# Second mixer: the state-space activation runs two passes later, the convolution's high part behind the tables, and one gate product ahead of the first linear part

## The reference

```python
y_ssm  = s5_mixer(u, ...)        # gelu(scan's output), then y @ w_glu: linear part and gate
y_conv = short_conv_mixer(...)   # (gate_b * causal_conv(gate_c * x)) @ w_out
y_attn = nsa_mixer(...)          # compressed, selected and windowed attention, @ w_o
gates  = sigmoid(mix_gates).reshape(bsz, seq, 3, D_MODEL)
mixed  = gates[:, :, 0] * y_ssm + gates[:, :, 1] * y_conv + gates[:, :, 2] * y_attn
x = x + mixed @ w_out
```

## Time and profile before

| what | us |
|---|---|
| time, median of 3 executions | 1519.97 (1518.13 to 1520.04) |
| profiled execution, its own time | 1513.86 |
| its span in the trace | 1511.9 |
| second mixer's passes and what follows up to `lin0`, in the trace | 1085 to 1234 |

### The profile page before, as it was taken

One profiled execution on the slowest core, in us unless ns is written; L12 is line 12 of the kernel. 1 busy time (PEld: TensorE's weight loads), 2 busy tenths in 40 slices (PEclk: granted clock), 3 DMA queues, 4 the chain that ended last, 5 costly groups with the idle time before them and its releaser, 6 DMA issues.

```text
span 1511.9 us, 24315 instructions
## 1 busy us (share of the span) xinstructions
PE 1464.1 (97%) x8495; PEld 1269.4 (84%) x8495; DVE 1146.9 (76%) x1836; ACT 771.6 (51%) x1257; POOL 140.1 (9%) x140
## 2 busy tenths in 40 slices
PE   6999999999999999999999999999999999999998
PEld 5888889888888888888978888798777789888887
DVE  4777777877777778777787777867599877568776
ACT  5443466563444543446655434467588665453432
POOL 0000015100000000004220000010332310000000
PEclk9999999999999999999999999999899999999999
DMA  7566545546565666565455665456222246646652
GB/s 294 196 196 195 191 148 175 154 152 193 197 194 187 208 204 188 191 194 152 142 167 190 195 194 187 167 172 227 98 84 70 85 145 190 186 156 193 195 192 81
DMA packets 71072, 261.74 MB, mean 173 GB/s; under 512 B 8016, under 2 KB 8016, under 8 KB 70736
## 3 DMA queue, kind: packets, MB, share of 16 engines
q1 hardware_dynamic: 69696, 253.79, 52.0%
q10 hardware_dynamic: 1296, 6.85, 1.3%
HBM read 259.56 MB, written 1.05 MB: 172 GB/s over the span
## 4 chain that ended last, share of the span: by engine, by line
PE 87%; DVE 6%; ACT 4%; issue 2%; POOL 1%; DMA 0%; DVEq 0%; ACTq 0%
PE work L733 24%; PE work L734 12%; PE work L469 8%; PE work L470 8%; PE work L471 8%; PE acc L469 7%; PE acc L471 7%; PE acc L470 7%; DVE wlo L455 2%; ACT whi L448 1%; PE work L1458 1%; PE acc L1487 0%; DVE x L572 0%; ACT xboth L526 0%; DVE frac L1868 0%
## 5 line engine op out<-in xcount | busy, mean ns | idle before, releaser
L455 DVE TENSOR_TENSOR wlo<-raw,whi 128x1024 fp32r<-128x1024 f32 x460 | 548.7, 1219 | 195.0 <-ACT whi L448 193.6
L733 PE MATMUL work<-xboth,whi 128*128 128x512 f32 x1600 | 560.7, 393 | 0.0
L448 ACT ACTIVATE whi<-raw 128x1024 fp32r<-128x1024 f32 x480 | 475.8, 1040 | 49.0 <-PE work L471 35.2
L734 PE MATMUL work<-xboth,wlo 128*128 128x256 f32 x1600 | 445.3, 278 | 0.0
L733 PEld LDWEIGHTS work<-xboth,whi 128*128 128x128 f32 x1600 | 299.7, 187 | 68.6
L734 PEld LDWEIGHTS work<-xboth,wlo 128*128 128x128 f32 x1600 | 301.1, 188 | 4.3
L813 ACT ACTIVATE sg<-sg 128x256 f32<-128x256 f32 x100 | 41.8, 418 | 476.0 <-DVE sg L854 476.0
L471 PE MATMUL acc<-whi,hlo 128*128 128x512 f32 x440 | 173.8, 395 | 0.0
L470 PE MATMUL acc<-wlo,hhi 128*128 128x512 f32 x440 | 173.6, 395 | 0.0
L469 PE MATMUL acc<-whi,hhi 128*128 128x512 f32 x440 | 173.5, 394 | 0.0
L469 PE MATMUL work<-xboth,whi 128*128 128x256 f32 x488 | 143.2, 293 | 0.0
(11 more groups left out here) (433 smaller groups left out, 2069.5 us busy)
## 6 DMA issues: line engine op xcount, KB each, us to landing
raw<-stream SPq DMA_DIRECT2D x480, 512.0 KB, 3.7
par<-pm ACTq DMA_DIRECT2D x2, 1644.5 KB, 7.3
pfa<-pf_a ACTq DMA_DIRECT2D x3, 516.0 KB, 3.9
pfb<-pf_b ACTq DMA_DIRECT2D x2, 516.0 KB, 8.1
x<-x_in SPq DMA_DIRECT2D x2, 512.0 KB, 5.8
out<-x SPq DMA_DIRECT2D x2, 512.0 KB, 2.6
par<-pm ACTq DMA_DIRECT2D x1, 820.0 KB, 4.7
pre<-pf_a ACTq DMA_DIRECT2D x1, 4.0 KB, 4.0
```

What stands on the lines that cost most here:

```text
L448: nc.scalar.activation(chunk(whi, place, c)[:, cols], chunk(raw, place, c)[:, cols], ACT.Copy).then_inc(hi_ready, 1)
L455: nc.vector.tensor_tensor(chunk(wlo, place, c)[:, cols], chunk(raw, place, c)[:, cols], chunk(whi, place, c)[:, cols].bitcast(F32), ALU.su ...
L733: nc.tensor.matmul(o[:, :], hi[:, k * P:(k + 1) * P], xboth[:, k, :], start=k == 0, stop=False)
L734: m = nc.tensor.matmul(o[:, 0:S], lo[:, k * P:(k + 1) * P], xhi[:, k, :], start=False, stop=k == KD - 1)
```

## The change

Three edits. `s5_gelu(k)` moves from the end of passes 4, 8 and 12 to passes 6, 10 and 14, where it stands behind the exponentials and ahead of the tables; DVE's `y5lo` moves with it, from passes 5, 9, 13 to 7, 11, 15. `cvhi` moves from behind the exponentials to behind the tables and the `cv` copy of the same pass. And `EARLY` takes in an 18th gate, e17, which is block (5, 2): PE computes it between `ot3` and `lin0`, into the spare bank, with its own copy, `split_hi` and `split_lo`; `g52` goes from the late part. The weight stream is re-ordered to match.

```diff
-EARLY = [(i, b) for i in range(KD) for b in range(3)][:17]
+EARLY = [(i, b) for i in range(KD) for b in range(3)][:18]
...
-BANKED2 += _tail + _ots
...
+BANKED2 += _tail + _ots + ["e17"]
...
+BY_ACT2 += _tail + ["e17"]
 BY_DVE2 += _ots
@@ mix2_pe
                 done(f"ot{b}", m)
+            early(17)
             for i in range(KD):
@@ mix2_act
                 emptied(f"sc{r}", ins)
-                if 3 <= r <= 12 and r % 3 == 0:
-                    vec2.wait(act, BY_DVE2.index(f"cv{r - 1}") + 1)
-                    cv_hi.inc(nc.scalar.activation(cvhi[:, r // 3 - 1, :], cvt[:, :], ACT.Copy))
                 if r == 0:
                     job2.wait(act, JOB2["pct"])
                     copy("pct", pcT[:, :, :].rearrange("p t n -> p (t n)"), bank2("pct", slice(0, S)))
+                if r >= 6 and r % 4 == 2:
+                    s5_gelu(r // 4 - 1)
                 if t == 0 and h + 1 < 8:
                     tables(h + 1)
...
+                if 3 <= r <= 12 and r % 3 == 0:
+                    vec2.wait(act, BY_DVE2.index(f"cv{r - 1}") + 1)
+                    cv_hi.inc(nc.scalar.activation(cvhi[:, r // 3 - 1, :], cvt[:, :], ACT.Copy))
                 split_hi(act, place, SPLIT_AFTER[r])
-                if r >= 4 and r % 4 == 0:
-                    s5_gelu(r // 4 - 1)
...
                 o_hi.inc(nc.scalar.activation(ohi[:, b, :], bank2(f"ot{b}", slice(0, S)), ACT.Copy))
+            early(17)
@@ mix2_dve
-                if r % 4 == 1 and r > 1:
+                if r % 4 == 3 and r > 4:
                     s5_low(r // 4 - 1)
...
                 emptied(f"ot{b}", ins)
+            split_lo(dve, place, [E_CHUNK[17] + 6])
```

More of the change, by code:

```diff
@@ L66 @@
 D_B = [D_ROUNDS + c for c in (3, 8, 13, 18)]
-E_CHUNK = [D_MIXED + c for c in (2, 5, 8, 11, 12, 13, 14, 15)] + [D_ROUNDS + c for c in (15, 16, 17, 19, 20, 21, 22, 23, 24)]
+E_CHUNK = [D_MIXED + c for c in (2, 5, 8, 11, 12, 13, 14, 15)] + [D_ROUNDS + c for c in (15, 16, 17, 19, 20, 21, 22, 23, 24, 25)]
 SPLIT_AFTER = {0: [6], 1: [7], 2: [8], 3: [9, 10], 4: [11], 5: [12], 6: [13], 7: [14, 15], 8: [16], 9: [17],
@@ L75 @@
     for _name in [f"g{_i}{_b}" for _b in range(3) if (_i, _b) not in EARLY] + [f"lin{_i}", f"br{_i}"]:
-        LATE[_name] = D_ROUNDS + 25 + len(LATE)
-D_PAD = D_ROUNDS + 25 + len(LATE)
+        LATE[_name] = D_ROUNDS + 26 + len(LATE)
+D_PAD = D_ROUNDS + 26 + len(LATE)
 D_OUT = D_PAD + 1
@@ L184 @@
 _tail = ["pt15", "e12", "e13", "e14", "e15", "e16"]
-BANKED2 += _tail + _ots
-BANK2.update(zip(_tail + _ots, [TURNED, CHANNEL, SPARE, SCORES, INPUTS, CHANNEL, TURNED, SCORES, INPUTS, CHANNEL]))
-BY_ACT2 += _tail
+BANKED2 += _tail + _ots + ["e17"]
+BANK2.update(zip(_tail + _ots + ["e17"], [TURNED, CHANNEL, SPARE, SCORES, INPUTS, CHANNEL, TURNED, SCORES, INPUTS, CHANNEL, SPARE]))
+BY_ACT2 += _tail + ["e17"]
 BY_DVE2 += _ots
@@ L325, in block_program @@
         gx = sb("gx", [P, 4, S])
-        gates32 += [gx[:, j, :] for j in range(3)] + [xn[:, t, 512:768] for t in range(T)]
+        gates32 += [gx[:, j, :] for j in range(3)] + [xn[:, t, 512:768] for t in range(T)] + [xn[:, 0, 768:D]]
         mxhi, mxlo = sb("mxhi", [P, KD, S], F32R), sb("mxlo", [P, KD, S], F32R)
@@ L2409, in mix2_chunks @@
     chunks.update(zip(E_CHUNK, [mg[b * KD + i] for i, b in EARLY]))
-    parts += [chunks[c] for c in range(D_MIXED, D_ROUNDS + 25)]
+    parts += [chunks[c] for c in range(D_MIXED, D_ROUNDS + 26)]
     def half(v, i):
```

## The result

Four executions of the changed kernel took 1507.78 to 1510.3 us, median 1509.57; four of the kernel before 1516.52 to 1520.04, median 1519.05. The ratio is 0.9939 (95% interval 0.9927 to 0.9952), 9.5 us by the medians. Measured again later beside 23 executions of the kernel before, it was 1511.04 against 1519.04, ratio 0.9946 (0.9933 to 0.9959), 8.0 us. The profiled execution of the changed kernel took 1507.78 us with a span of 1506.1, 6.1 us less than the profiled one of before. Of the 5.8 us between the spans, 3.9 us lie between nm(1) and `lin0` and 3.1 us behind `lin0`, less 1.2 us ahead of nm(1), where the changed kernel's execution was the later one.

What follows compares the result with a forecast made beforehand. DVE was taken to bound the middle passes and PE alone everything from `lin0` on. Gate 2.9 plus passes 4.9 gave 7.8 us, so 1519.97 - 7.8, say 1512 us, with a forecast range of 1510.5 to 1514.5 (chance 0.60).

Steps and rivals of the forecast that it cites:

- The bound and the gate: Ahead of `lin0`, where PE alone sets the time after: the gate fills the 3.19 us gap, worth 2.9 us, 3.2 at most.
- The last four us: Passes 12 to 15: DVE's 4.22 us wait for nm(15) goes; the passes give 3.4 to 5.5 us, 4.9 taken.
- The thin cover: Pass 14: exp(15) ends at 1205.2 to 1205.9, just ahead of PE's transposes at 1206.0; half a microsecond more would count.
- exp(13) comes 4.0 us earlier: End of pass 12: exp(13) starts at about 1190.2 instead of 1194.19, about 0.4 us behind nm(13).
- The expected price of pass 10: Three table loads: PE stands about 3.3 us in pass 11; half clock, likelier than not, costs pass 12 1.5 to 2.9 us.
- a sign of being wrong: Passes 8 and 12: a wait of DVE for scores(8) or scores(12) of over 1 us would show the prediction wrong.
- The early waits give nothing, DVE is busy there anyway: Passes 4 and 8: removing the early gelu's waits, and moving DVE's `y5lo` (0.4 us each), gains nothing.
- The difference of 6.11 us between the profiled execution and the median: Whole kernel: the profiled execution lay 6.11 us under the median; the same difference was set on the forecast median.
- more than forecast: Rival, whole kernel: clock stays up and unprofiled executions now lose more to late exponentials; 1508.5 to 1510 us, chance 0.06.
- `cvhi` as a term of its own: Pass 12: `cvhi` out of the way brings ACT's work up to the split 2.6 us earlier; no separate time gain given.
- The drain: ACT in passes 6 and 10: skill's rule of about 1380 ns per table switch, 4.1 us more each; left out of sum.
- slower with ACT as the bound: Rival, passes 6 and 10: ACT's list becomes the longest and delays DVE; with 5.5 us per pass, 1523 us, chance 0.06.

Runs made afterwards that it cites:

- e1: Only the 18th gate kept; activations and `cvhi` back in their old places, against the changed kernel; 1514.54 us against 1518.25 for the kernel before, ratio 0.9981.
- e2: The 18th gate put ahead of the transposes, so the wait for `olo` stays, activations and `cvhi` as before; 1520.85 us against 1518.25 before, ratio 1.0018.
- e3: The moves of all three activations and of `cvhi`, without the 18th gate (17 gates); 1514.96 us against 1518.25 before, ratio 0.9981.
- e4: Against the kernel before, 17 gates: `cvhi` moved and only the last activation moved, pass 12 to 14; 1515.04 us against 1518.25, ratio 0.9979.
- e8: Only the three activations moved against the kernel before, `cvhi` still behind the exponentials, 17 gates; 1517.75 us against 1519.04, ratio 0.9992.
- e9: The kernel before, unaltered, profiled a second time; 1518.71 us, span 1516.9, where its first profiled execution took 1513.86.
- e7: Only `cvhi` moved behind the tables against the kernel before, activations unmoved, 17 gates; 1518.77 us against 1519.04, ratio 0.9992.
- e5: The changed kernel unaltered, measured again beside the kernel before on the same chip; 1511.04 us against 1519.04, ratio 0.9946.
- e11: e10's version with `cvhi` back behind the exponentials; 1511.57 us against 1517.65 for the kernel before, ratio 0.9962.
- e6: The changed kernel with the three activations at the end of passes 5, 9 and 13, behind the split; 1507.58 us against 1519.04 before, ratio 0.9927.
- e10: The same version as e6, measured again; 1506.9 us against 1517.65 for the kernel before, ratio 0.9929.

## Why the prediction came out as it did

**The bound and the gate: right.** `lin0` waits 0.32 us where 0.3 were left over, the gate takes its place, and e1 and e2 show that the filled wait is what pays. The term of 2.9 us was measured at 2.9 to 3.7. Its upper bound of 3.2 left out the clock that may fall behind the gap: e2, e3, e4 and e8 had 1.4 to 2.4 us more to lose there, though neither profile of before had.

**The last four us: right in kind.** The 4.22 us wait of DVE went, scores(14) follow values(12) without a wait (1195.46 after 1194.97), the chain through POOL's rotation and the last `states_out` moved as one, and no wait appeared at the last transposes. The thin cover held: exp(15) end at 1209.1 and the transposes that need them start at 1209.46. The size in the profiled pair is 3.7 us from nm(1) to nm(15) (113.95 to 110.2) and 3.9 us from nm(1) to `lin0` (140.0 to 136.1), inside 3.4 to 5.5 and under the 4.9 taken, since the half clock behind PE's stand in pass 11 came in all three traces of this order (e3, the changed kernel twice). The stand itself was foreseen (3.3 us expected, 1.12 + 1.67 measured) and half clock was called likelier than not, yet the sum took a value near the end without it.

**"exp(13) comes 4.0 us earlier": not reached.** It starts 2.0 us behind the end of nm(13) (1194.01 against 1192.02), not 0.4. The expected price of pass 10 is the cause: with pass 12 at half clock, PE's transposes, not ACT, hold `pT`(12) (a wait of 2.48 us). In e4, where PE does not stand in pass 11, exp(13) comes 0.46 us behind nm(13), as forecast, and from nm(1) to nm(15) it takes 4.8 us less than e9. DVE is later in e3 than in e4 by 1.2 us from nm(11) to nm(15), where I had next to nothing: it waits 0.65 us for scores(12) and 1.03 us for the state inputs behind them. The prediction had named a wait of over 1 us there as a sign of being wrong.

**"The early waits give nothing, DVE is busy there anyway": wrong in most of the traces.** It was read from one execution, in which it was true. In four of the six traces of kernels that keep the early activations (e2, e4, e7 and e9; not in e1 and the first of before) the low clock behind PE's stands in passes 5 and 9 lasts longer, and DVE waits 0.9 to 1.1 us at nm(7) and 1.5 to 1.6 us at nm(11). In the first profiled pair the passes and the gate make 3.7 + 2.9 = 6.6 us. From e9 to the changed kernel it is 116.1 to 110.2 us, so 5.9 between nm(1) and nm(15), and with the gate's 2.9 it makes 8.8, against 8.0 and 9.5 measured. Moving those activations removed that wait, and put another in pass 12 in its place: 2.5 us less and 1.2 us more in e3 than in e4. The 0.7 us that are left of it at `lin0` are too little for the medians to show.

**The difference of 6.11 us between the profiled execution and the median: set on wholesale, and wrongly.** Some 2.2 us of it lie in the passes and are touched by the change. The rival "more than forecast" (1508.5 to 1510) named this, with 0.06, and the first median, 1509.57, lay in it; e5's 1511.04 lay in the forecast's own 1510.5 to 1514.5. That 7.8 us come so near to the measured 8.0 is in part luck: the price in pass 12 was set too low and the early waits at nothing, and the two errors work against each other.

**`cvhi` as a term of its own: mis-seen.** The prediction counted 2.6 us of ACT for it in pass 12 and put it with the activation into one term, without a price for either alone. In pass 6 it saw only that the gap for the convolution hides the activation. e7, e8 and e11 show that the two are alternatives in holding ACT: either alone keeps the exponentials late.

**The drain.** The Trainium skill (ScalarE: Activation LUTs, section What ACT_TABLE_LOAD costs) adds about 1380 ns of drain to each switch. No trace here shows it: the load of 1.28 us at 1206.80 begins 0.01 us behind the copy ahead of it (1206.40 and 0.39) and is followed by exp(15) at 1208.10. The rival that it would have fed, slower with ACT as the bound, did not come, and e6 is faster with two loads more.

What stays open: why the clock is low for longer in one execution than in the next, how often it falls behind the 3.2 us gap in the kernel before, and a second thing that differs between executions at full granted clock. In the 12 us from the first matmul of `lin0` on there are 106 matmuls in before, e9, e10, e11 and the first profile of the changed kernel, and 102 in e1, e5, e6 and e7, all at 1.00; of the kernels with 18 gates, those with 106 take 274.6 to 274.7 us from `lin0` to the end and those with 102 275.9 to 276.0.

## What to carry to other kernels

When an engine stands idle in a fixed place of a software pipeline, look at what another engine does just then, and put the work with its table load there, not where it first becomes possible: e6 and e10 gain 2 to 4 us over the change with two table loads more. Two items that both make the same instruction late have to be moved together; here each alone measured as 0.3 and 1.3 us, hardly told from nothing, and both as 3.3. And where the clock of TensorE moves between levels in the stretch in question, read two or three executions before a stall is called hidden: the slack that hides it may be smaller than the clock's share.

## What the runs showed of the hardware

A gap of 3.2 us on PE was followed by full clock in the profiled kernel before (1.00 in the 12 us behind it, 106 matmuls), and by 0.77 in e2 and 0.86 in e3, e4 and e8 (80 and 89 matmuls). PE's list around the gap is the same in before, e3, e4, e7 and e8; only e2's has the gate ahead of it. No kernel was seen going both ways at this gap: before kept the clock in both of its profiles. A pair of stands of 1.1 and 1.7 us was followed by a mean clock of 0.65 over the next 9 us in the changed kernel. One of 0.8 and 1.7 us ahead of scores(6) was followed by 0.85 over 11.6 us in one execution of the kernel before and by 0.75 over 12.8 us in another. So the price of a stand can't be read from one execution: here it lay between nothing and some 2.4 us above its length.
